# Six late weight loads of a hybrid decoder kernel, each cut into a piece of 120 and a piece of 8 partitions

## The chip, the core and the metric

The kernel runs on one core of a Trainium2 chip. The time is the device time of one execution in microseconds (us), as the median of three runs. One more execution was recorded by the hardware profiler; every row shown here comes from that one.

## What is computed

Two layers of a decoder on 512 tokens of width 1024, in float32. Each layer is a mixer (a projection `W_in`, four head groups, a projection `W_out`) and after it a channel mixer called PEER: every token is compared with 2 x 128 keys for each of 8 heads, the 16 best of 128 x 128 experts are taken per head, and each expert is one row of `peer_u` and one of `peer_v`:

```python
def hybrid_layer(x, ...):
    xn = rms_norm(x, norm1_g)
    z = xn @ w_in
    ...
    x = x + y @ w_out
    x = x + peer_ffn(rms_norm(x, norm2_g), w_query, sub_keys, peer_u, peer_v)

def peer_ffn(xn, w_query, sub_keys, peer_u, peer_v):
    q = (xt @ w_query).reshape(t, PEER_HEADS, 2, PEER_HALF)
    ...
    def block(args):
        xb, ib, gb = args
        h = jnp.einsum('thkd,td->thk', peer_u[ib], xb).astype(jnp.float32)
        a = (gb * jax.nn.gelu(h, approximate=False)).astype(xb.dtype)
        return jnp.einsum('thk,thkd->td', a, peer_v[ib])
```

So 512 tokens x 128 experts x 2 layers are fetched by index, and one fetched row (`peer_u` and `peer_v` side by side) has 2048 float32 numbers, 8192 bytes.

## The kernel before

The work is cut into four blocks `m` of 0 to 3 (`NBLK`): two layers, each in two halves of 256 tokens. A block's mixer and its query projection (`mixer_pe`, `mixer_act`, `mixer_dve`) are woven between the PEER chunks of the block before it by `interleave`, which is the same on TensorE (PE), VectorE (DVE) and ScalarE (ACT): it spreads the slices of `work(m + 1)` over the 64 chunks (`CHUNKS`) of block `m`. Block 3 has no mixer behind it, so its 64 chunks run alone at the end.

**The gathers.** GpSimd (POOL) issues 1024 indirect DMAs (L487), 16 for each of 64 groups of one head and one tile of 128 tokens. Each brings 128 rows of 8192 bytes, one into each partition, into one of 11 slots of `gather` (`SLOTS`). The gather `n` waits until the matmuls of gather `n - 11` have read its slot (`s_yc`) and signals `s_g[n % SLOTS]` with 16 increments. DVE (L1547) waits for all 16, multiplies the first half of the rows by the token's `xc` and sums; a chunk is four of these (`CH`). ACT makes a gelu (L1103) and four diagonals (L1110, L1118) of the sums, PE (L828) adds the second half of the rows into `ysum`. For the last chunk ACT goes gather by gather (`last_diagonals`, L1091 to L1097). Then DVE and ACT copy `ysum` to `x`, and SyncE (SP) stores it (L466).

**The weights.** SP loads the weight blocks two by two: `load_pair(n)` (L426 to L434) brings 2 blocks of [128, 8, 128] float32 into one of the two halves of `w`, which is 8192 bytes in each of 128 partitions, 1024 KB. Before the load of a pair SP waits (`ready`) for the matmuls that used the last block of the pair two before. Each half of `w` has a semaphore, `s_w[0]` and `s_w[1]`, to which a load adds 16. PE waits for it in `weights` (L532 of the new file, L511 of the old one):

```python
                n = W_AT[m, ("qa", name[1]) if name[0] == "qb" else name]
                pe.wait_ge(s_w[n % WS // 2], 16 * (n // WS + 1))
                return w[:, n % WS, :, :]
```

`WEIGHTS` lists all blocks in the order of use; the third entry of each is the number of the block in memory, of which 0 to 17 are `W_in`, 18 to 25 `W_out` and 26 to 41 the sixteen query blocks. The last entries of `WEIGHTS` are the query blocks of block 3, and the loads of these are the last ones before SP only waits to store the output. PE uses them at L548 (`project`), between the PEER chunks of block 2.

Of the kernel before, what the change touches and what calls it, by code (L numbers as in the profile page):

```python
# [27 lines left out]
P = 128  # L28
HALF = 256
TT = HALF // P  # L30
NBLK = 2 * DEPTH
# [8 lines left out]
WS = 4  # L40
# [7 lines left out]
NZ = 15  # L48
NV = 3
# [138 lines left out]
    JOB_NTH[_m, _name] = _by, 1 + sum(by == _by for by, _ in JOB_NTH.values())  # L188
WEIGHTS = [(m, name, w) for m, name, _, w in JOBS if w is not None]
W_AT = {(m, name): n for n, (m, name, _) in enumerate(WEIGHTS)}  # L190
W_FIRST = [next(n for n, (k, _, _) in enumerate(WEIGHTS) if k == m) for m in range(NBLK)]
BANKS = 6

# [29 lines left out]
def build(nc, x_d, wall_d, small_d, consts_d, g2b_d, late_d, uv_d, out_d):  # L223
# [3 lines left out]
    with ctx:  # L227
        def sb(name, *shape, dt=f32):
            return ctx.enter_context(nc.sbuf_tensor(name, [P, *shape], dt))

        def sem(name):
            return ctx.enter_context(nc.semaphore(name))
# [19 lines left out]
        w = sb("w", WS, KD, P)  # L252
# [58 lines left out]
        s_w = [sem(f"s_w{i}") for i in range(WS // 2)]  # L311
# [31 lines left out]
        def ready(eng, m, name):  # L343

            eng.wait_ge(s_ready, JOB_AT[m, name] + 1)
# [69 lines left out]
        block = ctx.enter_context(nc.Block())  # L415


        @block.sync
        def _(sp):
            x_t = x_d.rearrange("(t p) d -> p t d", p=P)  # L420
            sp.dma_start(x[:, 0, :], x_t[:, 0, :]).then_inc(s_xin[0], 16)
            sp.dma_start(cc[:, 0:CC_HEAD], consts_d[:, 0:CC_HEAD]).then_inc(s_head, 16)
            sp.dma_start(x[:, 1, :], x_t[:, 1, :]).then_inc(s_xin[1], 16)
            sp.dma_start(small[:, :, :], small_d).then_inc(s_small, 16)

            def load_pair(n):  # L426


                m, _, b = WEIGHTS[n]
                if n >= WS:  # L430

                    em, ename, _ = WEIGHTS[n - WS + 1]
                    ready(sp, em, ("qb", 1) if ename == ("qa", 1) else ename)
                sp.dma_start(w[:, n % WS:n % WS + 2, :, :], wall_d[m // 2, b // 2]).then_inc(s_w[n % WS // 2], 16)  # L434

            for n in range(0, WS, 2):
                load_pair(n)
            sp.dma_start(cc[:, CC_HEAD:CC_N], consts_d[:, CC_HEAD:CC_N]).then_inc(s_const, 16)
            sp.dma_start(late[:, :, :], late_d[0]).then_inc(s_late, 16)
            sp.dma_start(g2b[:, :], g2b_d[0]).then_inc(s_g2b, 16)  # L440
            sp.dma_start(x[:, TT:, :], x_t[:, TT:, :]).then_inc(s_xrest, 16)
            for n in range(WS, len(WEIGHTS), 2):
                load_pair(n)
                m = WEIGHTS[n][0]
                b = n - W_FIRST[m]
                if m == 0 and b in (8, 10, 12, 14):

                    i = b - 8
                    sp.dma_start(gather[:, WO + i // 2, :].rearrange("p (b c k) -> p b c k", b=2, c=KD),
                                 wall_d[0, (NZ + NV + i) // 2]).then_inc(s_wout, 16)  # L450
                if m == 0 and b == 16:

                    sp.dma_start(wheld, wall_d[0, (NZ + NV + 8 + 2) // 2]).then_inc(s_wheld, 16)
                if m and m % 2 == 0 and b == WS:

                    ready(sp, m - 1, ("sk", 1, HEADS - 1))
                    sp.dma_start(late[:, :, :], late_d[m // 2]).then_inc(s_late, 16)
                if m and m % 2 == 0 and b == NZ + NV + 12:

                    sp.wait_ge(s_h, (m - 1) * CHUNKS + CHUNKS // 2 + 1)  # L460
                    sp.dma_start(g2b[:, :], g2b_d[m // 2]).then_inc(s_g2b, 16)
            first = SEQ // P * (DEPTH - 1)
            for t in range(SEQ // P):

                sp.wait_ge(s_x, 2 * (first + t + 1))
                sp.dma_start(out_d[t * P:(t + 1) * P, :], x[:, t, :]).then_inc(s_out, 16)  # L466
            sp.wait_ge(s_out, 16 * (SEQ // P))
# [25 lines left out]
        def mixer_pe(pe, m):  # L493
# [11 lines left out]
            def weights(name):  # L505

                if name[0] in ("qa", "qb") and name[1] >= 2:
                    pe.wait_ge(s_wheld, 16)
                    return wheld[:, name[1] - 2, :, :]
                n = W_AT[m, ("qa", name[1]) if name[0] == "qb" else name]  # L510
                pe.wait_ge(s_w[n % WS // 2], 16 * (n // WS + 1))  # L511
                return w[:, n % WS, :, :]

            def transpose_half(kind, t, h, src):
# [28 lines left out]
            def project(name, tokens=slice(0, HALF)):  # L543

                wt = weights(name)
                ps = start(name)
                for d in range(KD):
                    mm = nc.tensor.matmul(ps[:, tokens], wt[:, d, :], xnT[:, d, tokens], start=d == 0, stop=d == KD - 1)  # L548
                mm.then_inc(s_ready, 1)
# [41 lines left out]
            for i in range(NORMED + NV):  # L591
                if i < NORMED:
                    project(("z", i))
                else:
                    wt = weights(("v", i - NORMED))
                    ps = start(("v", i - NORMED))
                    for t in range(TT):
                        for d in range(KD):
                            mm = nc.tensor.matmul(ps[:, t * P:(t + 1) * P], xnT[:, d, t * P:(t + 1) * P], wt[:, d, :],  # L599
                                                  start=d == 0, stop=d == KD - 1)  # L600
                    mm.then_inc(s_ready, 1)
                if i == NORMED:
                    if m == 0:
                        pe.wait_ge(s_const, 16)
                    sum_squares(("zs", 0), range(NORMED))
                if i == NORMED + NV - 1:
                    for j in range(4):
                        spread(("zb", j), 3 * m + 1, range(2 * j, min(2 * j + 2, NORMED)))
                yield
# [180 lines left out]
            for i in range(8):  # L790
                wt = weights(("out", i))
                ps = start(("out", i))
                for t in range(TT):
                    for n, c in enumerate(YORDER):
                        if i == t == 0 and n == 6:
                            done(pe, m, ("yb", 3))
                        mm = nc.tensor.matmul(ps[:, t * P:(t + 1) * P], yT[:, c, t * P:(t + 1) * P], wt[:, c, :],  # L797
                                              start=n == 0, stop=n == 7)
                mm.then_inc(s_ready, 1)
                yield  # L800
# [900 lines left out]
```

## Time and profile before

| | |
|---|---|
| median of 3 runs | 2903.8 us (2902.21 to 2904.62) |
| the profiled execution, its own time | 2906.1 us |
| its span | 2904.3 us |
| PE, DVE, ACT, POOL busy | 2075.9, 2051.7, 1068.7, 1218.9 us |
| moved by DMA | 1171.17 MB, of which 1073.81 MB by the queue of the gathers |

The profile has a page with the busy times, the span in 40 slices, the DMA queues and a chain of work that ended last, and views of stretches, waits and single instructions that are cut from the same record. A core has 16 DMA engines; the views give them together, as a mean share of the 16 that was busy and as GB/s. No view tells the engines apart. The share is taken from the durations of packets, which overlap a little, so that a share of 1.01 is 16 busy engines. In a stretch in which exactly one of 16 is busy the share is 1/16, printed as 0.06.

### The profile page before, as it was taken

The page shows a single profiled execution, that of the slowest core. Times are in us where ns is not written, and L with a number is a line of the kernel's source. Part 1 is how long each engine was busy: PE and PEld are TensorE (multiplying, and loading weights), DVE is VectorE, ACT ScalarE, POOL GpSimd, SP SyncE. Part 2 cuts the span into 40 slices and gives each one's busy share as a digit, 9 for nine tenths or more (in the row PEclk, how much of TensorE's full clock was granted, in tenths as well). Part 3 has the DMA queues.
Part 4 walks back from the last instruction along what each step waited for, and adds up shares of the span by engine and source line. Part 5 has one row for each costly group of instructions (what it writes and reads, how often), then busy time and mean ns, then how long its engine had stood idle before and what let it go on. Part 6 is the DMA issues. An engine that isn't in the chain of part 4 may idle for free.

```text
span 2904.3 us, 37407 instructions
## 1 busy us (share of the span) xinstructions
PE 2075.9 (71%) x12792; PEld 1031.8 (36%) x12792; DVE 2051.7 (71%) x5222; ACT 1068.7 (37%) x3378; POOL 1218.9 (42%) x1028
## 2 busy tenths in 40 slices
PE   8988788687777776686766877666776566555555
PEld 7654444244433432243432533224343111111111
DVE  3665679976667788866658678886757766677665
ACT  2433346633243355423224345632323322222222
POOL 0044434443344444444444454354444444444443
PEclk9998999898989998898887988888898767776777
DMA  6399999999999999999999999999999999999998
GB/s 229 114 421 421 421 404 421 421 421 402 421 422 420 421 421 421 416 421 421 421 419 409 421 421 416 392 421 421 421 421 420 417 419 417 420 410 420 417 419 332
DMA packets 161887, 1171.17 MB, mean 403 GB/s; under 512 B 17952, under 2 KB 18208, under 8 KB 19872
## 3 DMA queue, kind: packets, MB, share of 16 engines
q0 software_dynamic: 147456, 1073.81, 89.3%
q1 hardware_dynamic: 14240, 94.97, 8.1%
q8 instruction: 101, 1.65, 0.2%
q14 instruction: 90, 0.74, 0.1%
HBM read 1166.61 MB, written 2.10 MB: 402 GB/s over the span
## 4 chain that ended last, share of the span: by engine, by line
DMA 57%; PE 17%; DVE 16%; issue 5%; ACT 4%; POOL 0%; SPq 0%; DVEq 0%; POOLq 0%; ACTq 0%
DMA gather<-experts,idx 56%; DVE gather L1547 9%; PE ysum L828 9%; PE bank L548 6%; ACT amp L1110 2%; ACT diag L1118 1%; ACT gel L1103 1%; PE ysum L557 1%; DVE shared L1267 1%; PE bank L599 0%; DVE top_i L1444 0%; DVE top_i L1441 0%; PE bank L625 0%; DVE scratch L1472 0%; DVE scratch L1476 0%
## 5 line engine op out<-in xcount | busy, mean ns | idle before, releaser
L487 POOL DMA_INDIRECT gather<-experts,idx x1024 | 1218.7, 1190 | 1663.4 <-PE ysum L828 1293.7
L828 PE MATMUL ysum<-gather,diag 64*64 64x512 f32 x8192 | 1236.5, 755 | 713.7 <-ACT diag L1118 708.8
L1547 DVE CUSTOM_DVE_ANT_0 gather<-gather,xc 128x1024 f32<-128x1024 f32 x1024 | 1230.1, 1224 | 693.3 <-DMA gather<-experts,idx 658.6
L828 PEld LDWEIGHTS ysum<-gather,diag 64*64 64x64 f32 x8192 | 361.0, 169 | 1495.6 <-ACT diag L1118 921.3
L1103 ACT ACTIVATE gel<-hdot 128x4 f32<-128x4 f32 x255 | 52.4, 205 | 1612.1 <-DVE hdot L1547 1582.7
L548 PE MATMUL bank<-xnT,w 128*128 128x256 f32 (+1 forms) x1984 | 460.0, 388 | 7.3 <-DVE xnT L1188 7.3
L548 PEld LDWEIGHTS bank<-xnT,w 128*128 128x128 f32 x1984 | 373.6, 195 | 100.6 <-issue 43.1
L1118 ACT ACTIVATE diag<-cc,amp 128x64 f32<-128x64 f32 x1020 | 268.4, 333 | 2.2 <-PE ysum L828 2.2
L1110 ACT ACTIVATE amp<-gel,gate 128x1 f32<-128x1 f32 x1020 | 216.9, 283 | 8.3
L1103 ACT ACT_TABLE_LOAD x112 | 143.7, 1283 | 2.0
L797 PEld LDWEIGHTS bank<-w,yT 128*128 128x128 f32 x768 | 87.2, 192 | 17.0 <-issue 17.0
L797 PE MATMUL bank<-w,yT 128*128 128x128 f32 x768 | 91.1, 278 | 0.0
L1547 DVE DVE_READ_ACCUMULATOR2_ANT hdot<- 128x1 f32 x1024 | 83.8, 82 | 0.0
L1082 ACT ACT_TABLE_LOAD x64 | 82.1, 1283 | 1.1
L883 ACT ACTIVATE shared<-bank 128x256 f32<-128x256 f32 (+1 forms) x108 | 38.7, 363 | 81.0 <-PE bank L548 80.7
L700 PE MATMUL bank<-late,shared 128*128 128x128 f32 x252 | 40.1, 302 | 34.0 <-ACT shared L883 34.0
L931 ACT ACTIVATE shared<-shared,st 128x256 f32<-128x256 f32 (+3 forms) x96 | 50.6, 528 | 19.1 <-issue 8.4
L700 PEld LDWEIGHTS bank<-late,shared 128*128 128x128 f32 x252 | 33.0, 202 | 57.9 <-ACT shared L883 34.9
L1267 DVE CUSTOM_DVE_ANT_0 shared<-bank,cc 128x256 f32<-128x256 f32 (+3 forms) x96 | 41.1, 453 | 16.5 <-PE bank L625 16.2
L931 ACT ACT_TABLE_LOAD x38 | 48.8, 1283 | 0.7
L599 PEld LDWEIGHTS bank<-w,xnT 128*128 128x128 f32 x384 | 44.0, 192 | 5.6 <-issue 5.3
L1472 DVE TENSOR_TENSOR scratch<-pos_f,cc 128x512 f32<-128x512 f32 x63 | 43.6, 692 | 2.2
(153 smaller groups left out, 1475.5 us busy)
## 6 DMA issues: line engine op xcount, KB each, us to landing
w<-weights SPq DMA_DIRECT2D x79, 1024.0 KB
gather<-experts,idx POOLq DMA_INDIRECT x1024
gather<-weights SPq DMA_DIRECT2D x4, 1024.0 KB, 6.9
y_out<-x SPq DMA_DIRECT2D x4, 512.0 KB
x<-x_in SPq DMA_DIRECT2D x2, 512.0 KB, 4.2
g2b<-g_rows SPq DMA_DIRECT2D x2, 512.0 KB
x<-x_in SPq DMA_DIRECT2D x1, 1024.0 KB, 12.9
scores<-weights SPq DMA_DIRECT2D x1, 1024.0 KB, 6.9
```

The source lines that it names most:

```text
L487: pool.indirect_dma_start(gather[:, n % SLOTS, :], None, uv_d[m // 2], bass.IndirectOffsetOnAxis(ap=idx[:, g % 2, k:k + 1], axis=0)).then_ ...
L548: mm = nc.tensor.matmul(ps[:, tokens], wt[:, d, :], xnT[:, d, tokens], start=d == 0, stop=d == KD - 1)
L700: mm = nc.tensor.matmul(ps[:, k * P:(k + 1) * P], qT[:, hc, t * P:(t + 1) * P], skt[:, k, :], start=True, stop=True)
L797: mm = nc.tensor.matmul(ps[:, t * P:(t + 1) * P], yT[:, c, t * P:(t + 1) * P], wt[:, c, :], start=n == 0, stop=n == 7)
L828: mm = nc.tensor.matmul(ysum[outs, q * 512:(q + 1) * 512], diag[toks, n % NDIAG, :], gather[toks, n % SLOTS, DM + hf * 512:DM + (hf + 1) * ...
L931: e = nc.scalar.activation(at[:, s, mp, 0:cols], at[:, s, mp, 0:cols], ACT.Exp, bias=st[:, s, 2 + mp:3 + mp], scale=scale, accum_out=st[:, ...
L1082: nc.scalar.activation(gate_e[:, :], best_v[:, :], ACT.Exp, bias=neg_best[:, :], accum_out=gate_s[:, 0:1]).then_inc(s_ge, 1)
L1103: nc.scalar.activation(gel[:, c % 2, :], hdot[:, c % 2, :], ACT.Gelu).then_inc(s_gl, 1)
L1110: nc.scalar.activation(amp[:, c % 2, j:j + 1], gel[:, c % 2, j:j + 1], ACT.Copy, scale=gate[:, c // 4 % 2, k:k + 1]).then_inc(s_a, 1)
L1118: nc.scalar.activation(diag[:, n % NDIAG, :], ident64, ACT.Copy, scale=amp[:, c % 2, j:j + 1]).then_inc(s_dg, 1)
L1267: V.tensor_tensor_reduce(out=at[:, s, mp, 0:cols], in0=bank_of(m, ("s", a, mp))[:, 0:cols], in1=bias, scale=1.0, scalar=-BIG, op0=ALU.add, ...
L1547: e = V.tensor_tensor_reduce(out=gather[:, n % SLOTS, 0:DM], in0=gather[:, n % SLOTS, 0:DM], in1=xc[:, :], scale=1.0, scalar=0.0, op0=ALU. ...
```

## The change

Loads for which `spared(n)` holds go in two DMAs, one of partitions 0 to 119 and one of partitions 120 to 127, instead of one of 128 partitions. `spared` holds for block 3 and for the memory blocks from 15 + 3 + 8 + 4 = 30 on, which are the query blocks 4 to 15 of the last half of the last layer: six pairs. The two DMAs add to the same semaphore, 16 each, and `landed(n)` counts for PE how much the semaphore must have when a pair is in. Nothing else differs.

```diff
+MOST = 120
+
+
+def spared(n):
+
+
+    return WEIGHTS[n][0] == NBLK - 1 and WEIGHTS[n][2] >= NZ + NV + 8 + 4
+
+
+def landed(n):
+
+
+    return 16 * sum(1 + spared(i) for i in range(n % WS // 2 * 2, n + 1, WS))
+
...
-                sp.dma_start(w[:, n % WS:n % WS + 2, :, :], wall_d[m // 2, b // 2]).then_inc(s_w[n % WS // 2], 16)
+                room, block = w[:, n % WS:n % WS + 2, :, :], wall_d[m // 2, b // 2]
+                if spared(n):
+
+                    sp.dma_start(room[0:MOST], block[0:MOST]).then_inc(s_w[n % WS // 2], 16)
+                    sp.dma_start(room[MOST:P], block[MOST:P]).then_inc(s_w[n % WS // 2], 16)
+                else:
+                    sp.dma_start(room, block).then_inc(s_w[n % WS // 2], 16)
...
-                pe.wait_ge(s_w[n % WS // 2], 16 * (n // WS + 1))
+                pe.wait_ge(s_w[n % WS // 2], landed(n))
```

The instructions of SP, the only engine on which any are added, at the end of its program before. `w` is the room for the weights, `weights` their place in memory, and 128x2048 is partitions by float32 numbers:

```order
L434 DMA w<-weights 128x2048 [waits s_ready] x13
L461 DMA g2b<-g_rows 128x1024 [waits s_h]
L434 DMA w<-weights 128x2048 [waits s_ready] x26
L466 DMA y_out<-x 128x1024 [waits s_x] x4
L227 UNCONDITIONAL_BRANCH [waits s_out]
```

The same place with the change:

```order
L482 DMA g2b<-g_rows 128x1024 [waits s_h]
L455 DMA w<-weights 128x2048 [waits s_ready] x20
L452 DMA w<-weights 120x2048 [waits s_ready]
L453 DMA w<-weights 8x2048
L452 DMA w<-weights 120x2048 [waits s_ready]
L453 DMA w<-weights 8x2048
L452 DMA w<-weights 120x2048 [waits s_ready]
L453 DMA w<-weights 8x2048
```

Three more such pairs of rows follow, then the stores. Of the last 26 loads 20 stay whole, and each of the other six is now two DMAs, the second of which follows the first without a wait.

## Rows read from the trace of the kernel before

**Rows 1.** The page: DMA busy tenths and GB/s in 40 slices, and the queues.

```profile
DMA  6399999999999999999999999999999999999998
GB/s 229 114 421 421 421 404 421 421 421 402 421 422 420 421 421 421 416 421 421 421 419 409 421 421 416 392 421 421 421 421 420 417 419 417 420 410 420 417 419 332
...
q0 software_dynamic: 147456, 1073.81, 89.3%
q1 hardware_dynamic: 14240, 94.97, 8.1%
```

**Rows 2.** The page: shares of the chain that ended last, by engine.

```profile
DMA 57%; PE 17%; DVE 16%; issue 5%; ACT 4%; POOL 0%; SPq 0%; DVEq 0%; POOLq 0%; ACTq 0%
```

**Rows 3.** Windows of 200 us: busy of PE, PEld, DVE, ACT, POOL; PEclk, DMA share, GB/s.

```profile
1000.00:1200.00 200.00, 142.41 (x876) 64.26 (x868) 167.76 (x475) 104.79 (x302) 95.77 (x76) 0.85 1.01 420
...
2000.00:2200.00 200.00, 149.72 (x921) 80.51 (x914) 132.71 (x324) 60.79 (x203) 85.79 (x72) 0.88 1.01 421
2200.00:2400.00 200.00, 120.37 (x701) 39.72 (x703) 140.70 (x340) 60.42 (x214) 92.98 (x79) 0.76 1.01 418
2400.00:2600.00 200.00, 113.14 (x644) 32.08 (x640) 140.72 (x340) 55.55 (x202) 95.09 (x80) 0.76 1.01 415
```

**Rows 4.** Windows at the end, same columns.

```profile
2885.00:2886.00 1.00, 0.70 (x8) 0.00 (x0) 0.39 (x2) 0.00 (x0) 0.00 (x0) 1.00 1.00 418
...
2887.00:2887.50 0.50, 0.00 (x0) 0.00 (x0) 0.50 (x1) 0.00 (x0) 0.00 (x0) 1.00 0.83 344
2887.50:2888.00 0.50, 0.00 (x0) 0.00 (x0) 0.37 (x2) 0.10 (x1) 0.00 (x0) 1.00 0.58 246
2888.00:2888.50 0.50, 0.00 (x0) 0.00 (x0) 0.00 (x0) 0.47 (x3) 0.00 (x0) 0.75 0.36 148
2888.50:2889.00 0.50, 0.00 (x0) 0.00 (x0) 0.00 (x0) 0.50 (x4) 0.00 (x0) 0.50 0.12 49
2889.00:2889.50 0.50, 0.21 (x4) 0.21 (x8) 0.29 (x1) 0.50 (x3) 0.00 (x0) 0.50 0.04 16
2889.50:2892.00 2.50, 2.50 (x16) 0.68 (x16) 1.38 (x3) 1.29 (x5) 0.00 (x0) 0.50 0.06 26
2893.00:2894.00 1.00, 1.00 (x8) 0.25 (x5) 0.00 (x0) 0.68 (x3) 0.00 (x0) 0.50 0.06 25
2895.00:2896.00 1.00, 1.00 (x12) 0.29 (x8) 0.26 (x2) 0.64 (x3) 0.00 (x0) 0.96 0.06 25
2896.00:2896.50 0.50, 0.50 (x11) 0.15 (x6) 0.01 (x1) 0.20 (x1) 0.00 (x0) 1.00 0.00 0
```

**Rows 5.** The chain that ended last, its final stretch: start, duration, what.

```profile
2881.61 14.86 DMA gather<-experts,idx
2896.47 0.02 issue
2896.49 1.22 DVE gather L1547
```

**Rows 6.** The timeline of SP: first and fifth of the last six weight loads.

```profile
2064.55 0.33 SPq L434 DMA_DIRECT2D w<-weights  x1
...
2152.98 17.09 SPq L434 DMA_DIRECT2D w<-weights  x2
```

**Rows 7.** The timeline of PE: L548 for the blocks of the fifth of these pairs.

```profile
2173.79 3.62 PE L548 MATMUL bank<-xnT,w 128*128 128x256 f32 x16
2183.38 3.72 PE L548 MATMUL bank<-xnT,w 128*128 128x256 f32 x16
```

**Rows 8.** The waits of SP from 1990 to 2190: total, times, longest.

```profile
SPq L434 <- PE bank L548: 145.3, 6, 41.8
SPq L434 <- PE bank L797: 36.0, 2, 23.8
```

## The prediction, made before the changed kernel ran

> **What bounds the kernel now.** I read the slices and queues of the profile's page first [rows 1]. From the fourth slice on the 16 DMA engines are busy nine tenths or more and move about 421 GB/s, and most of it is the queue of the gathers: 1073.81 of 1171.17 MB. The chain that ended last says the same: 57% of it is DMA [rows 2]. The windows of 200 us make it sharper [rows 3]: a DMA share of 1.01 in each, with PE and DVE at 142 and 168 us of 200 in the busiest shown and lower later. The DMA engines have work without a break, so the time is the work of a DMA engine, plus the first 150 us and a short tail. The reader should look at which of the 16 ends last, and by how much.
>
> No view names a DMA engine, but the end shows them one by one [rows 4]. Until 2887.0 all 16 work. Then the share falls, 0.83, 0.58, 0.36, 0.12 in steps of half a microsecond, and from 2889.0 to 2896.0 it is 0.06 at 25 or 26 GB/s: 1/16, one engine alone. The others have nothing left because POOL issued the last gather at 2881.61, and it landed at 2896.47, 14.86 us later [rows 5]; DVE starts on it at once. So **one engine lags behind the other fifteen by 7.0 us**, and the chain goes through it.
>
> **What the change does, in numbers.** A gather of 1,048,576 bytes at 421 GB/s takes 2.49 us, 8 rows on each engine, so a row of 8192 bytes takes an engine 0.311 us (311 ns x 26.3 GB/s, which the lone engine's 25 or 26 GB/s confirms [rows 4]). A pair of weight blocks is 128 such rows too, 8 per engine.
>
> 1. Relief. If the last engine has no share in six pairs, it is spared 6 x 8 = 48 rows, 48 x 0.311 = 14.9 us, between 2064.55 and the load after 2152.98 [rows 6]. It lags by 7.0, so it would then end about 8 us ahead of the others, and the fifteen set the end. The most to be had from this is 7.0 us, not 14.9.
> 2. What the others get. 120 rows on fifteen engines are 8 for each, as before. The piece of 8 partitions is 8 rows more per pair. One row each on eight engines costs each of these 6 x 0.311 = 1.9 us; the bounds are 0 (they fall where there is room) and all eight on one engine, 48 rows or 14.9 us. I take one row each, by the even sharing of all loads so far. At 2888.25 the mean share was 0.36, some 5 or 6 engines, one of them the laggard, and at 2888.75 it was 0.12, two [rows 4]. Of four or five late engines one in the eight is all but sure, so the fifteen end between 2888.3 + 1.9 and 2888.9 + 1.9, or 2890.2 to 2890.8, against 2896.0 now.
> 3. Gain: 2896.0 - 2890.5 = **5.5 us** (5.2 to 5.8, and 7.0 if no row counts). The tail behind the last landing, DVE's 1.22 us and then ACT, PE and the store, stays the same.
> 4. Gathers that land earlier release their slots earlier. In the windows after 2200 the rate is 418 and 415 GB/s against 421 [rows 3]; a piece of this could be fast engines short of work while their slots wait for the laggard. 1% of 700 us is 7 us, the upper bound, and 0 the lower. With the share printed at 1.01 I take 0 in the sum and allow 1 to 2 us in the range.
> 5. SP issues 6 DMAs more, 0.33 us each [rows 6], and sits in waits for 181 of 200 us there [rows 8]: nothing, covered by these waits. Behind the second piece is only the next load's wait for PE. If the cover were gone, it would be 2 us.
> 6. PE's wait now needs both pieces. The fifth pair is issued at 2152.98 and its first block used at 2173.79 [rows 6, 7], 20.8 us later. A load and the gathers that share the engines evenly with it would take about 2 x 2.49 us, and one row more 0.3: nothing, with some 15 us left. If it were late, PE's weight matmuls would be late behind it in its order, and the chunk's diagonals after them.
>
> POOL, DVE and ACT keep every instruction. No other part of the span, and above all not the 700 us behind the last weight, does anything differently, other than that the gathers come with a smaller spread.
>
> Sum, against the profiled execution: 2906.1 - 5.5 = 2900.6. It was 2.3 us above the median of the runs shown, and in those the lag may differ; I keep the difference: 2903.8 - 5.5 = **2898.3 us**. That is 0.19%. About 0.2%, or 5.8 us, is what a measurement of this kernel can tell from no change, so even the forecast sits on the edge of it.
>
> **Which engine, and how it is shared out.** The lone engine at the end [rows 4] has no number, and the sum rests on its being the one that is spared. The Trainium skill, DMA: Bandwidth & Descriptors, section Latency and other measured facts, says that engines 7 and 15 of 16 are usually slower than the rest; the trace shows one laggard, not two. By that page's section on why a DMA increments its semaphore by 16, a load by SP uses the largest number of engines up to 16 that divides its partitions, the lowest-numbered ones: 15 for 120 and 8 for 8. By it engine 15 is spared and engine 7 gets the extra row, which is the sum above; if the laggard is 7, the change makes it worse by 1.9 us.
>
> **The rivals.**
>
> *The lagging engine is not the spared one, or is not spared.* For it: no view gives its number, and the change is written as if the number were known. Against: nothing in the rows. The end stays with the laggard: 2903.8 if it gets no row more, 2905.7 if it gets six. Chance 0.19.
>
> *The pieces get in each other's way (slower).* All loads so far were over 128 partitions, and rows 3 show them at full rate beside gathers, 421 GB/s between 2000 and 2200. A piece of 120 cannot be laid over engines and partitions in the same pattern, so engines will write where another engine's gather rows go. If two rows meet and share the rate of one, each takes 0.62 us instead of 0.31. With all 9 rows of a pair on an engine meeting another: 54 x 0.311 = 16.8 us more for each of the fifteen. They end at 2888.9 + 1.9 + 16.8 = 2907.6 instead of 2896.0, +11.6 us, or 2915.4. It decides against the change when the loss is over 5.2 us, a third of that. Chance 0.12, with half of it between 2905 and 2910. The trace has no such transfer, neither for nor against. The Trainium skill, SBUF — State Buffer, section Door 1: The DMA port swizzle, has this as its rule: 16 ports of about 27.2 GB/s, each for eight partitions that are not neighbours, and a DMA is as fast as its ports. The trace's 421/16 = 26.3 GB/s for an engine is just under one such port. By it the six small pieces, on two ports, are the worst places.
>
> *120 rows go to fewer engines.* If eight take 15 rows each and one of the small piece, that is 8 rows more per pair, 14.9 us, for engines that now end by 2888.9: 2903.8 against 2896.0, +7.8 us, 2911.6. The even share of all 128-partition loads speaks neither way. Chance 0.08.
>
> *It brings more.* The lag in runs without the profiler is larger, or the released slots bring back part of the 1% of term 4: 8 to 10 us, 2894 to 2896. Chance 0.09.
>
> **How the numbers follow.** The forecast, relief of 5.2 to 7.0 us with up to 2 us either side for the state of the lag in another execution, has 0.52 and its own range is 2895.5 to 2900.5. I predict 2898.3. Low 2895.0 leaves out half of the last rival, some 0.05. High 2909.0 takes in the forecast, the first rival, and the milder part of the collisions; it leaves out the rest of these and the fewer engines, some 0.14. Faster by over 0.2%: 0.29 of the forecast and 0.09 are 0.38. Within 0.2%: 0.23 and the first rival's 0.19 are 0.42. Slower: 0.12 + 0.08 = 0.20.
>
> **What would show it right or wrong.** Right: at the end the share falls from 1.0 to 0 within 3 or 4 us with no stretch of 0.06 for seven, the last landing comes 5 to 6 us earlier, and the last gather's wait falls from 14.86 to about 9 us. The rate between 2064 and 2200 stays at 421 GB/s. First rival: the lone stretch of 0.06 is as long as before or 2 us longer. Collisions: the rate in 2060 to 2200 drops, by 16.8 us of 140 at worst, that is to some 370 GB/s, while the lone stretch is gone. Fewer engines: a long stretch at the end with a share near 0.5. I am wrong in the sum if the fifteen engines' end, not the laggard's, has moved by more than 2 us; I am wrong about the cover if PE waits for a DMA before a matmul of L569, the new line of L548.

## The result, and the profile after

The changed kernel takes 2932.8 us against 2903.8 us, 29.0 us more: the ratio is 1.0096 with a 95% interval of 1.0085 to 1.0106. The profiled execution has a span of 2931.0 us against 2904.3. The forecast was 2898.3 and its range ended at 2909.0.

The page of the profile after says where the time went before any other view is opened. Here are its GB/s in 40 slices and its two queues, which answer to [rows 1]:

```profile
GB/s 238 125 421 421 421 404 421 417 420 402 421 421 420 421 421 421 417 421 420 421 419 409 421 421 412 399 421 421 358 326 413 412 421 417 417 418 416 418 417 334
...
q0 software_dynamic: 147456, 1073.81, 89.1%
q1 hardware_dynamic: 14282, 94.97, 8.3%
```

From the third slice on all are within 10 of those of before but two, which fell from 421 to 358 and 326; they are 73 us each, from 2052 to 2198. The bytes are the same, and q1, the queue of SP's loads, has 42 packets more: 14282 for 14240. Each engine that takes part in a load ends its share with one small packet. A load over 16 engines has 16, beside its 128 rows; six times (15 + 8 - 16) is 42, which fits pieces that run on 15 and on 8 engines.

The windows of 40 us of the kernel before, columns as in [rows 3]:

```profile
2020.00:2060.00 40.00, 26.75 (x177) 12.58 (x180) 27.62 (x70) 16.52 (x49) 16.06 (x16) 0.79 1.01 422
2060.00:2100.00 40.00, 29.88 (x183) 16.69 (x172) 24.01 (x58) 8.57 (x38) 18.06 (x15) 0.91 1.01 421
```

The same of the kernel after:

```profile
2020.00:2060.00 40.00, 25.59 (x169) 11.48 (x158) 28.48 (x71) 14.54 (x41) 15.84 (x15) 0.83 1.01 421
2060.00:2100.00 40.00, 27.10 (x161) 15.02 (x159) 18.67 (x46) 7.20 (x31) 14.78 (x14) 0.87 1.02 346
2100.00:2140.00 40.00, 23.67 (x132) 10.88 (x132) 18.86 (x41) 10.53 (x36) 12.42 (x11) 0.74 1.00 352
2140.00:2180.00 40.00, 29.82 (x169) 16.95 (x166) 22.60 (x58) 10.76 (x36) 15.11 (x14) 0.87 1.01 350
2180.00:2220.00 40.00, 24.84 (x141) 13.69 (x143) 19.37 (x53) 8.61 (x33) 8.89 (x9) 0.83 1.00 342
2220.00:2260.00 40.00, 29.34 (x200) 15.53 (x196) 27.53 (x69) 12.62 (x47) 18.37 (x17) 0.91 1.01 416
```

Read the last two columns together. The share stays at 1.00 to 1.02, so the engines are as busy as before, but they move 342 to 352 GB/s in place of 421. They are not short of work: rows take longer. In the 160 us from 2060 to 2220 that is 160 x (1 - 347.5/421) = 27.9 us of lost transfer, nearly all of the 29.

Which rows? The DMA queues of that stretch, of the kernel before (columns: packets, MB, share of 16 engines):

```profile
q0 software_dynamic: 8284, 60.32, 90.7%
q1 hardware_dynamic: 1008, 6.82, 10.2%
```

and of the kernel after:

```profile
q0 software_dynamic: 6686, 48.69, 84.2%
q1 hardware_dynamic: 1050, 6.82, 16.5%
```

The stretch has 16 x 160 = 2560 us of engine time. 6.82 MB are the six loads and one store, in all as much as 832 rows of 8192 bytes: the rows of this queue took 0.102 x 2560 / 832 = 0.314 us each before and 0.165 x 2560 / 832 = 0.508 us after. The gathers' rows, 7363 and 5944 of them, took 0.315 and 0.363 us. The rows of SP's queue lost 832 x 0.194 = 161 us and the gathers' 5944 x 0.0473 = 281 us, together 442 us of engine time, 27.6 us for each of 16. So the gathers, which the change does not touch, carry almost two thirds of the loss.

The means hide what happens to one row. The packets beneath the views have a duration each, and I counted those of 8192 bytes from 2060 to 2220. Before, all 768 rows of the loads and all but 12 of 7373 rows of the gathers took 0.29 to 0.33 us. After, 4891 of 5956 rows of the gathers still did, and 729 of the others took 0.48 to 0.66; of the 768 rows of the loads 43 did, and 567 took 0.48 to 0.66. Most rows are as before or take 1.5 to 2 times as long, as if two shared the rate of one.

The end of the span, columns as in [rows 4], shows the other half of the story:

```profile
2914.00:2915.00 1.00, 0.00 (x0) 0.00 (x0) 0.56 (x2) 0.37 (x2) 0.00 (x0) 0.50 0.67 279
2915.00:2916.00 1.00, 0.03 (x4) 0.03 (x4) 0.11 (x1) 1.00 (x6) 0.00 (x0) 0.50 0.12 49
2916.00:2920.00 4.00, 4.00 (x20) 1.27 (x24) 2.36 (x4) 1.96 (x8) 0.00 (x0) 0.50 0.07 29
2920.00:2922.00 2.00, 2.00 (x20) 0.68 (x16) 1.24 (x2) 0.41 (x3) 0.00 (x0) 0.81 0.07 29
2922.00:2923.00 1.00, 1.00 (x12) 0.29 (x8) 0.00 (x0) 0.81 (x3) 0.00 (x0) 1.00 0.04 16
```

One engine alone works from 2916 to some way into the last of these, 6 to 7 us, much as before. The chain's last wait answers to [rows 5]:

```profile
2908.30 14.83 DMA gather<-experts,idx
```

14.83 us for 14.86. The laggard is still there.

SP's timeline [rows 6] shows no cost of issue: the third of the six, as the others, goes out in two DMAs of 0.3 to 0.4 us.

```profile
2116.55 0.33 SPq L452 DMA_DIRECT2D w<-weights  x1
2116.92 0.30 SPq L453 DMA_DIRECT2D w<-weights  x1
```

Beneath the views the trace has the increments of each gather's semaphore, sixteen where none is missing from the record, and I read them as one from each engine. Five gathers of the kernel after that have all sixteen: the first increment in us from the span's start, and how much later the 2nd, 3rd, 14th, 15th and 16th came.

```
2054.7:  0.0  0.2  0.2 ...  1.7  2.2  7.5    before the first cut load
2077.1:  0.0  2.2  2.4 ...  3.8  4.1  9.8    after it
2100.6:  0.0  5.8  6.0 ...  7.4  7.9 13.4    after the second
2207.8:  0.0  5.3  5.6 ...  8.4  9.4 14.9    after the sixth
2221.0:  0.0  0.2  0.4 ...  3.4  3.6  9.2    13 us later
```

An engine runs ahead of the others after the cut loads; the spared one has 8 rows less each time, so I take it to be that one. In these five the last stays 5.3 to 5.7 us behind the one before it: it is another engine. The lead of the first, 5.3 us at 2207.8, is gone at 2221.0. The next gathers can't be issued before slots come free, which may be why; no row here shows that one engine stood idle.

### The profile page after: what moved, and what is told of

The parts are those of the page before. It is cut to its first block, busy times and chain, and to the rows that moved or that the text cites. A ratio compares the mean times of both kernels' runs of the same rounds, so it can differ in the third digit from the quotient of the medians.

```text
span 2931.0 us, 37413 instructions
## 1 busy us (share of the span) xinstructions
PE 2076.5 (71%) x12792; PEld 1033.9 (35%) x12792; DVE 2051.9 (70%) x5222; ACT 1069.1 (36%) x3378; POOL 1214.7 (41%) x1028
## 3 DMA queue, kind: packets, MB, share of 16 engines
q1 hardware_dynamic: 14282, 94.97, 8.3%
## 4 chain that ended last, share of the span: by engine, by line
DMA 57%; PE 17%; DVE 16%; issue 5%; ACT 4%; POOL 0%; SPq 0%; DVEq 0%; POOLq 0%; ACTq 0%
DMA gather<-experts,idx 57%; DVE gather L1568 9%; PE ysum L849 8%; PE bank L569 5%; ACT amp L1131 2%; ACT diag L1139 1%; PE ysum L578 1%; ACT gel L1124 1%; DVE shared L1288 0%; DVE top_i L1465 0%; DVE top_i L1462 0%; PE bank L646 0%; PE bank L620 0%; DVE top_v L1464 0%; PE bank L721 0%
## 5 line engine op out<-in xcount | busy, mean ns | idle before, releaser
L569 PE MATMUL bank<-xnT,w 128*128 128x256 f32 (+1 forms) x1984 | 459.0, 387 | 8.7 <-DVE xnT L1209 8.7
L569 PEld LDWEIGHTS bank<-xnT,w 128*128 128x128 f32 x1984 | 372.8, 194 | 102.4 <-issue 43.8
```

## The experiments

Two theories stood after this. **Meeting**: a piece of a load over fewer than 128 partitions sends rows of one engine to places in SBUF, the core's memory of 128 partitions, where other engines' rows go, and both are slowed. **Overhead**: two DMAs for one, or an uneven share of engines, are what costs. Beside these stood the question of the laggard. Each kernel was measured beside the kernel before, the ratio is to that, and as it is estimated from all executions it can differ by 0.06% from that of the medians.

### Two DMAs over all partitions

```diff
-                    sp.dma_start(room[0:MOST], block[0:MOST]).then_inc(s_w[n % WS // 2], 16)
-                    sp.dma_start(room[MOST:P], block[MOST:P]).then_inc(s_w[n % WS // 2], 16)
+                    sp.dma_start(room[:, 0:1], block[:, 0:1]).then_inc(s_w[n % WS // 2], 16)
+                    sp.dma_start(room[:, 1:2], block[:, 1:2]).then_inc(s_w[n % WS // 2], 16)
```

> The six loads go in two DMAs each as in the changed kernel, but cut along the free dimension: one block of 128 x 4096 bytes and then the other, so that every DMA covers all 128 partitions. If the loss of 29 us comes from rows of different engines meeting in the same place of SBUF, this is free: 2901 to 2907 us, and no dip of the rate between 2060 and 2220. If it comes from two DMAs in place of one (issue, semaphore, queue order), it stays near 2932 us.

Measured: a ratio of 1.0002 (0.9993 to 1.0012), 2907.0 us against 2904.8, the time of before. Its window, columns as above:

```profile
2060.00:2100.00 40.00, 28.26 (x172) 14.89 (x176) 24.10 (x63) 12.22 (x46) 16.38 (x15) 0.90 1.02 419
```

419 GB/s, no dip, and 419 to 422 in the three windows that follow. Neither the second DMA nor two on one semaphore costs anything that shows; of Overhead the uneven share is left.

### The big piece alone

```diff
                 if spared(n):
                     sp.dma_start(room[0:MOST], block[0:MOST]).then_inc(s_w[n % WS // 2], 16)
-                    sp.dma_start(room[MOST:P], block[MOST:P]).then_inc(s_w[n % WS // 2], 16)
```

`landed(n)` counts 16 for each load, as before. The kernel leaves rows 120 to 127 of these weight blocks unloaded.

> Only the piece of 120 partitions is loaded in the six late pairs; the piece of 8 is left out, so that rows 120 to 127 of these weight blocks are those of an earlier pair. If the big piece's rows meet rows of other engines, most of the loss stays: 4 us of the 4.8 us per pair, 2922 to 2930 us. If the small piece is the costly one (eight engines writing into few places at once), 2898 to 2908 us.

Measured: 1.0067 (1.0050 to 1.0083), 2925.1 us. The median is 20 us above that of the kernel before, measured beside it. Its q1 has 54 packets less than before, 6 x (8 rows + 1): the big piece runs on 15 engines. It carries about 20 of the 29 us, the small one the rest, some 1.5 us for each set of 8 rows.

### A cut that spares no engine

```diff
-MOST = 120
+MOST = 112
```

> The same cut at partition 112: 7 rows and then 1 row on each of 16 engines, if the engines share both pieces evenly, so that none is spared and none has more than another. If rows meeting is the cause, it is slow all the same: 2915 to 2930 us. If the cause is the uneven share (15 engines and then 8), it is the time of before, 2901 to 2907 us.

Measured: 1.0059 (1.0042 to 1.0075), 2923.1 us. Its q1 has 14336 packets, 96 more than before, 6 x 16: both pieces run on all 16 engines. The median is 18 us above that of before. So an uneven share is not needed for the loss; a cut of the partitions is enough.

### Half as many cut loads

```diff
-    return WEIGHTS[n][0] == NBLK - 1 and WEIGHTS[n][2] >= NZ + NV + 8 + 4
+    return WEIGHTS[n][0] == NBLK - 1 and WEIGHTS[n][2] >= NZ + NV + 8 + 10
```

> Only the last three pairs are cut in 120 and 8. If each cut load costs the same, 4.8 us, the time is half way: 2916 to 2920 us. The lone stretch at the end (DMA share 0.06), 7 us before, says whether the laggard is the engine that is spared: 24 rows or 7.5 us of relief would take it away if it is; it stays at 6 to 8 us if another engine lags.

Measured: 1.0046 (1.0030 to 1.0063), 2919.9 us, 15 us above before. The cost goes with the number of cut loads, 5 us each. Two windows of its end, just before the last row lands, have about one engine at work, as in the other kernels:

```profile
2908.80:2909.80 1.00, 1.00 (x12) 0.31 (x8) 0.31 (x1) 0.37 (x2) 0.00 (x0) 0.92 0.09 33
2909.80:2910.80 1.00, 1.00 (x15) 0.32 (x10) 0.92 (x2) 0.04 (x1) 0.00 (x0) 1.00 0.06 25
```

With 24 rows of relief, 7.5 us, one engine still ends alone.

### Cut in the middle

```diff
-MOST = 120
+MOST = 64
```

> The changed kernel with the cut at partition 64. If a piece of 64 partitions is shared by 16 engines, 4 rows each, whose places in SBUF are those of 8 engines' gathers, rows meet again and the loss is of the size of the other cuts, 10 to 25 us. If each engine takes the rows of the partitions that it also writes for the gathers, a piece uses 8 engines, nothing meets and the time is that of before, 2901 to 2907 us.

Measured: 1.0072 (1.0057 to 1.0087), 2928.1 us. It too has 14336 packets in q1, so a piece of 64 partitions is spread over 16 engines. The loss is the one that Meeting expects of that.

### Cut loads without any gather beside them

```diff
+                    if i == 0:
+                        sp.dma_start(slot, part).then_inc(s_wout, 16)
+                    elif i == 2:
+                        sp.dma_start(slot[0:120], part[0:120]).then_inc(s_wout, 16)
+                        sp.dma_start(slot[120:P], part[120:P]).then_inc(s_wout, 16)
+                    elif i == 4:
+                        sp.dma_start(slot[0:64], part[0:64]).then_inc(s_wout, 16)
+                        sp.dma_start(slot[64:P], part[64:P]).then_inc(s_wout, 16)
+                    else:
+                        sp.dma_start(slot[:, 0:1], part[:, 0:1]).then_inc(s_wout, 16)
+                        sp.dma_start(slot[:, 1:2], part[:, 1:2]).then_inc(s_wout, 16)
```

> The kernel before, with its four loads of W_out into the gather slots (37 to 63 us, before any gather) cut in four ways: whole, 120 and 8 partitions, 64 and 64 partitions, and two halves of the free dimension. No gather runs then, so the time stays that of before. If rows of one load already meet one another, the piece of 120 and the pieces of 64 take longer from issue to landing than the whole load's 6.9 us although no gather is beside them, by 1 to 4 us; the free halves do not. If rows only meet those of the gathers, all are near 6.9 us.

One execution, 2903.9 us. The view gives no time to landing for these loads, so I read the q1 row of the DMA view in four stretches, each of which has one whole load of `w` and then one of the four, 2.10 MB in all: 34.5 to 41 (whole), 41.5 to 51 (120 and 8), 51.5 to 60 (64 and 64), 60.5 to 69 (free halves).

```profile
q1 hardware_dynamic: 277, 2.10, 80.6%
...
q1 hardware_dynamic: 295, 2.10, 76.3%
...
q1 hardware_dynamic: 292, 2.10, 87.2%
...
q1 hardware_dynamic: 435, 2.10, 65.6%
```

Share x 16 x length is the engine time: 83.8, 116.0, 118.6 and 89.2 us. The two whole loads cost 83.8; with a cut one it is 32 to 35 us more, 2.0 to 2.2 us for each engine, and with free halves 5 (its rows are twice as many and half as long). So rows of one cut load already slow one another, with no gather near, and take about 1.8 times as long as those of a whole load, (116.0 - 41.9) / 41.9. The packets' own durations agree. Of the last 128 rows of each stretch the median is 0.309 us for the whole load, 0.593 for the cut at 120, 0.611 for the cut at 64, and 0.159 for the half rows.

### Who is the laggard?

What finds it is work that goes to a known number of engines and to no partition at all: copies from the weights in memory to the output's place in memory, behind the last weight load. The output is written over them later, and SP waits for them first.

```diff
+            for i in range(4):
+                sp.dma_start(spare[16 * i:16 * i + 15], rows(wall_d[0, i])[0:15]).then_inc(s_extra, 16)
+            sp.wait_ge(s_extra, 64)
```

`spare` and `rows` are the output and a pair of weight blocks as rows of 32 KB. Three kernels, with 15, 8 and 7 rows:

> The kernel before, and behind its last weight load SP issues four DMAs from the weights in memory to the output's place in memory (overwritten by the real output later), each 15 rows of 32 KB: 16 rows of 8192 bytes more for each of the engines that such a DMA uses, 16 x 0.311 = 5.0 us, with no partition of SBUF in it. If it uses the lowest 15 engines and the laggard is the sixteenth, the time stays within 1 us of before and the lone stretch at the end shrinks from 7 to about 2 us. If the laggard is one of the 15, +5 us and a lone stretch of 7 us or more.

> The same with 8 rows of 32 KB per DMA, so 16 rows of 8192 bytes more for each of 8 engines. If the laggard is among these eight, +5 us and a lone stretch of about 12 us or a stretch that is unchanged in length against seven others; if it is among the other eight, the time of before within 1 us and the lone stretch shrinks to about 2 us.

> The same with 7 rows of 32 KB per DMA, on 7 engines. If e6 was slower and this is not, the laggard is the eighth engine (number 7); if both are slower it is among the first seven; if neither is, among the last eight.

(`e6` there is the kernel with 8 rows.)

Measured: 1.0016 (1.0007 to 1.0025), 1.0012 (1.0003 to 1.0021) and 1.0007 (0.9998 to 1.0016). These told nothing of which engine is the laggard. All three have 14368 packets in q1, 128 more than before: the rows lie one behind the other in memory, and the DMA was shared by 16 engines whatever their number. Each engine got 15, 8 or 7 rows of 8192 bytes more, 4.7, 2.5 and 2.2 us, and the medians rose by 4.4, 3.5 and 0.7; the interval of the last takes in no change at all.

With a gap behind each row they can't be joined:

```diff
+            for rep in range(2):
+                for i in range(4):
+                    sp.dma_start(spare[16 * i:16 * i + 15, 0:7 * DM], rows(wall_d[0, i])[0:15, 0:7 * DM]).then_inc(s_extra, 16)
+                sp.wait_ge(s_extra, 64 * (rep + 1))
```

> Which engine lags. Extra DMAs from memory to memory as in the run with 15 rows of 32 KB, which turned out to be shared by all 16 engines because the rows joined to one piece; here each row is 28 KB with a gap of 4 KB behind it, so that the 15 rows can't be joined. Eight such DMAs are 28 rows of 8192 bytes, 8.7 us, more for each of 15 engines. If the sixteenth engine is the laggard it ends as before and the fifteen end 8.7 later, 1.7 us after it: 2904 to 2908 us, and no lone stretch but one of many engines. If the laggard is one of the fifteen, +8.7 us (2911 to 2915) with a lone stretch of 7 us or more.

> The same with 8 rows, on 8 engines, 8.7 us more for each of these. If the laggard is one of the eight: 2911 to 2915 us and a long lone stretch. If it is one of the other eight: 2904 to 2908 us and no lone stretch. Together with the run on 15 engines this puts the laggard in one of three groups.

> The extra rows from memory to memory, 28 rows of 8192 bytes or 8.7 us for each engine used, now on 7 engines. The runs on 15 and on 8 were both 8 us slower, so the laggard is among the lowest eight. If it is the eighth (number 7), it has no row more here: 2904 to 2908 us, and the lone stretch is short or gone. If it is one of the lowest seven, 2911 to 2915 us as before, with a lone stretch of 6 to 8 us.

> 28 extra rows from memory to memory, 8.7 us, on 5 engines. The runs on 15, 8 and 7 engines were all about 8 us slower, so the laggard is among the lowest seven (0 to 6). If it is one of 0 to 4: +8 us, 2911 to 2915. If it is 5 or 6: the five loaded ones end at 2889 + 8.7, about 2 us behind the laggard, 2904 to 2908 us.

> 28 extra rows on the lowest 4 engines. 2 and 3 engines cost nothing (ratio 0.9998), 5 cost 8 us, so the laggard is the fourth or the fifth of the order in which such a DMA takes its engines. +8 us and a lone stretch of 7 us: it is the fourth (number 3). No loss and a stretch of four or five engines at the end: the fifth (number 4).

> The same on 3 engines: +8 us if the laggard is 0, 1 or 2; +1 to 3 us if it is 3 or higher.

> The same on 2 engines: +8 us if the laggard is 0 or 1; +1 to 3 us if it is 2 or higher. If all three of these runs are +8 us, either engine 0 or 1 lags, or the rule of adding 8.7 us does not need the laggard at all, and any engine that gets 28 rows more costs 8 us; then the lone stretch at the end tells which: it would be made of the loaded engines.

The packets of q1 say how many engines each took part with: 240, 128, 112, 80, 64, 48 and 32 more than before, 8 DMAs x 2 packets x 15, 8, 7, 5, 4, 3 and 2. The times:

```
engines   ratio to before    interval
15        1.0026             1.0015 to 1.0036
 8        1.0029             1.0019 to 1.0040
 7        1.0033             1.0023 to 1.0042
 5        1.0030             1.0018 to 1.0041
 4        1.0038             1.0023 to 1.0053
 3        0.9998             0.9988 to 1.0007
 2        0.9998             0.9988 to 1.0007
```

The same 8.7 us of extra work costs 8 to 10 us on four engines or more, and nothing on three or two. By the times alone it could also be the number of engines that decides. The increments of the gathers' semaphores rule that out. These are the last seven of sixteen, in us after the first, for a gather that landed before the extra rows (2160 to 2164 us) and one that landed behind almost all of them (2192 to 2195):

```
engines  before the extra rows                  behind them
2        2.7 3.1 3.2 3.2 3.4 3.4  9.0     3.2 3.3 3.4 3.4  9.5 10.1 13.1
3        1.9 2.1 2.3 4.0 4.3 4.5  8.9     3.9 4.3 4.5  9.9 10.1 10.4 12.4
4        2.2 2.7 3.1 3.2 3.3 3.3  8.2     3.0 3.1 4.0  9.5 10.5 13.4 17.7
5        2.1 2.3 3.1 3.3 3.3 3.6  9.1     3.6 3.6  9.7 10.3 10.4 12.4 20.0
```

Behind the extra rows k engines stand apart at the end of the line when k is 4 or 5, and k + 1 when it is 2 or 3. The last of them is at 17.7 and 20.0 us in the first case and at 13.1 and 12.4 in the second. So the laggard is among the four and not among the three: it is the fourth engine in the order in which SP's DMAs take them. Where the time goes shows in the rate, with 3 engines loaded and then with 4:

```profile
2200.00:2220.00 20.00, 13.93 (x92) 6.96 (x92) 9.74 (x18) 4.92 (x21) 9.08 (x8) 0.91 1.01 413
...
2200.00:2220.00 20.00, 16.01 (x96) 8.69 (x92) 11.65 (x22) 5.86 (x23) 11.16 (x8) 0.90 0.92 360
```

With the laggard loaded the share falls to 0.92: other engines stand idle, and its extra work is paid there, not at the end. With 2 engines loaded there are two at work at the end, not one, until 2892.5. The second is probably a loaded engine that has not caught up:

```profile
2887.50:2888.50 1.00, 0.98 (x8) 0.38 (x12) 1.00 (x1) 0.68 (x3) 0.00 (x0) 0.50 0.12 49
2888.50:2889.50 1.00, 1.00 (x12) 0.39 (x8) 0.18 (x2) 0.50 (x2) 0.00 (x0) 0.50 0.14 57
...
2891.50:2892.50 1.00, 1.00 (x16) 0.30 (x12) 0.24 (x1) 0.43 (x2) 0.00 (x0) 1.00 0.13 49
2892.50:2893.50 1.00, 1.00 (x16) 0.41 (x12) 0.99 (x2) 0.00 (x0) 0.00 (x0) 1.00 0.06 25
```

With 4 loaded it is alone again at the end, 6.0 us behind the next by the increments of the last gather.

These runs also weigh against a rival that is otherwise open. A cut changes not only which engine writes a partition but also which engine reads which row of the weights in memory, and no run here separates the two. But extra rows on 15 engines, read from memory and written to memory, took 0.305 us per 8192 bytes, and all but 3 of 645 gathers' rows beside them took less than 0.33. So 15 engines at work in place of 16 slow nothing by themselves. That the rows meet in SBUF is thus the account that fits every run, but it is argued; shown is that a cut of the partitions makes rows slow one another.

## Why the prediction was wrong

**What bounds the kernel**: right. 16 engines work without a break, one of them 7 us behind the rest, and 27.6 of the 29.0 us are found in the durations of the DMA rows.

**Step 1, the relief, failed**, where it took the engine that ends last for the one that is spared. One engine was spared, but the laggard is another: it still ends 6.2 us behind the next, and the relief of 5.5 us is 0. By the runs with extra rows it is the fourth, if the chips agree, and since these DMAs take the engines from the first on, only a piece on three engines or fewer would leave it out. That was the first rival, at 0.19. The text saw that the rows don't number the engines and still gave it less than half the weight of the forecast. The Trainium skill, DMA: Bandwidth & Descriptors, section Latency and other measured facts, says that engines 7 and 15 are usually slower. By the Trainium skill, the same page, section Why a DMA increments its semaphore by 16 and not by 1, SP's DMAs take the lowest-numbered engines; if so, the runs with 2 to 15 engines show neither 7 nor 15 as the laggard here.

**Step 2, what the others get, failed in its price**, and this is where the 29 us come from. The sharing was right: 120 rows on 15 engines and 8 on 8, by 42 packets more. But the sum took every row at 0.311 us and put nothing for rows that slow one another, so it had 1.9 us for the others. Measured, the loads' rows took 0.508 us and the gathers' 0.363, 27.6 us for each engine. By the Trainium skill, DMA: Bandwidth & Descriptors, section Why a DMA increments its semaphore by 16 and not by 1, the number of engines is the largest up to 16 that divides the rows; every count here agrees, if rows that lie one behind the other are taken as one piece.

**Steps 3 and 4** fell with the first. That the gain can't exceed the lag was not tested: no load of this kind leaves the fourth engine out. The 8.7 us that two or three engines took at no cost are the only direct sight of the room that the others have.

**Steps 5 and 6, SP's issue and PE's wait**: right. In the kernel with free halves the same number of DMAs and the same waits cost nothing, and in the changed kernel PE never waits for a DMA before L569.

**The rival that came true**, the pieces in each other's way, had the mechanism and the place right, with full engines and a rate of 421 down to about 370 GB/s at worst; it was 342 to 352, and the lone stretch, which this rival had as gone, stayed. It had a chance of 0.12 and a price of 16.8 us per engine at most. Its term counted the pieces' rows alone: 54 of them, each delayed by one row's time. Measured, those rows went from 0.314 to 0.508 us, 10 us per engine with the few other rows of that queue, less than feared. But a meeting has two sides, and the gathers' rows lost 17.6 us per engine, which the term left out. The statement that "the most to be had" is bounded by 7 us was made for the gain, and nothing of the kind was looked for on the other side. The range ended at 2909 because only half of that rival's chance was let in; but its worst case, 2915.4 us, lies 17 us short of the measured time too. It also took the relief of step 1 for granted. The Trainium skill, SBUF — State Buffer, section Door 1: The DMA port swizzle, has the rate follow the number of ports that the partitions reach. By its formula the pieces of 64 and of 8 partitions reach few ports, but the piece of 120 reaches all 16, and it alone cost 20 us. So the number of ports reached doesn't give the price. The prediction's own argument, that engines write where another engine's rows go, fits all four cuts; no run here sees a port.

**Fewer engines for 120 rows**: did not happen.

## What to carry to other kernels

Beside DMA engines that never rest, don't cut a transfer along the partitions: 1 MB in two pieces of partitions cost 3 to 5 us here, and in two halves of the free dimension nothing. In the cut at 120 most of the price was paid by the other transfers. Before giving one engine less, find out which one is late: extra DMAs from memory to memory with k rows, separated by a gap, load k engines, and a few runs with different k give the place of the late one in their order. Work on the late engine is paid in full, 8 to 10 us for 8.7 here, and the same work on two or three others cost nothing.

## What the runs showed of the hardware

Rows of a load cut at partition 120 or 64 slow one another with no gather running: 0.58 to 0.60 us a row in the mean in place of 0.33, 0.593 and 0.611 in place of 0.309 in the median (the stretches from 34.5 to 60 us). A busy share of 1.0 is no proof of full speed; it was 1.00 to 1.02 at 342 to 352 GB/s as at 421.

One engine ends 5 to 7 us behind the next in every profile taken here but those with 2 and 3 engines loaded, where a second one is 2 to 3 us before it. The runs with 5, 4, 3 and 2 engines, all on one chip, name the fourth; those with 15, 8 and 7 and gaps, on another chip, only say that it is among the lowest seven, and the profile of the changed kernel only that it is not the spared one. Why it lags is open. In the kernel before, by the increments of the semaphores, the last was level with the next at 300 us, 7 behind at 1850, 3 behind at 1883 after a dip of the rate, 5 at 2050 and 7 again from 2400 on.
